# Seven instead of eight block products for three pairs of feed-forward blocks, in a two-model kernel on one core

## The chip, the cores and the metric

The kernel runs on one core of a Trainium2 chip. What counts is the time of one execution on the device in microseconds (us), as the median of several runs. The core has TensorE (matmuls, PE in the profile), VectorE (DVE), ScalarE (ACT), GpSimd (POOL) and SyncE (SP), which here only issues loads. Each engine works through its own list of instructions in order and waits on semaphores for the others.

## The reference

The input is x with 256 tokens of 1024 features, all in float32. Two models are run one after the other: a block with a gated delta rule beside sliding-window attention, then a feed-forward network; and two layers, one with a short convolution and one with dilated attention, each followed by a feed-forward network; a norm ends it. The three feed-forward networks (FFN 0, 1 and 2 below) are what the change touches. Each has a hidden width of 2816:

```
h   = rms_norm(x) * weight                 # 256 tokens x 1024
ffn = (silu(h @ w_gate) * (h @ w_up)) @ w_down
x   = x + ffn                              # FFN 0: x + gate2 * ffn
```

## The kernel before

**Three matmuls for one product.** Every float32 operand is split in two parts of a shorter format (fp32r): high = copy(value), low = value - high. A product is high*high + high*low + low*high, three matmuls into one bank of PSUM. Activations are split once. Weights are split as they arrive: ScalarE's `hi(w)` (L706) copies a tile of 128x2048 from `raw` to `w_hi`, VectorE's `lo(w)` (L1121) subtracts into `w_lo`.

**Loads.** The weights lie in one stream of blocks of 1 MB (128x2048). `raw` has three slots. SyncE's load number i waits until load i-3 has been consumed (`lo_ready`, or `mod_accumulated` for blocks that belong to the modulation of the first model) and then fills its slot. The split tiles have five places: slots 0, 1, 2 in `w_hi`/`w_lo` and 3, 4 in `w_hi2`/`w_lo2`; `FORMER` names the tile whose matmuls must be over (`block_used`) before `hi(w)` may overwrite a place.

**An FFN.** The hidden width is cut in 11 blocks j of 256. For a block, `gate_up(f, j, t)` computes gate and up columns side by side (512 columns) for each half t of the tokens: 8 pieces k of the contraction, 3 matmuls each, so 24 matmuls of 512 columns into bank B[t]. ScalarE applies silu (L968), VectorE multiplies with up (L1598 or L1601). `turn_hid` transposes the result (4 PE instructions, L2371) into bank B[2], ScalarE and VectorE split it (`hid_high` L973, `hid_low` L1606), and `token_rows` multiplies it with block j of w_down: 24 matmuls of 512 columns. The order on TensorE is gate_up(j, 0), gate_up(j, 1), down block j-1 with turn_hid(j) in its middle. The weight tiles of block j+1 are split meanwhile: `lo` on VectorE goes down j-1, gate j+1, product, up j+1, product, hid_low. In FFN 0 VectorE also adds up four more blocks of the stream (`accumulate`, L1143 to L1147), their column sums on TensorE make the last modulation (gate2).

GpSimd does little in the FFNs; at the start of FFN 0 its queue loads two tables for the dilated attention (`t5`, L670 and L671), which the attention after FFN 1 reads.

## Time and profile before

| | |
|---|---|
| median of 3 runs | 980.93 us (980.77 to 981.27) |
| the profiled execution, its time | 981.34 us |
| its span in the trace | 979.5 us |
| PE busy | 971.1 us, 99% |
| DVE busy | 602.9 us, 62% |
| ACT busy | 476.6 us, 49% |
| FFN 0, 1, 2 begin at about | 203, 492 and 790 us of the span |

Busy time says how long an engine had an instruction in work; the granted TensorE clock was full (1.00) in the FFNs. The two numbers of the profiled execution differ by what lies outside of the first and last instruction, 1.8 us.

### The profile page before, as it was taken

How to read it: one execution, taken by the hardware profiler on the slowest of the kernel's cores; microseconds unless marked ns; L12 is line 12 of the kernel's file. 1: busy time of each engine (PE TensorE's matmuls, PEld its weight loads, DVE VectorE, ACT ScalarE, POOL GpSimd, SP SyncE). 2: the span in 40 equal slices, each digit the busy share in tenths (PEclk: the TensorE clock that was granted, in tenths of full speed). 3: DMA queues.
4: the chain of work that ended last, by engine and by line, in shares of the span. 5: the costliest groups of instructions: out<-in, count | busy, mean ns of one | idle time of the engine just before them, and what ended most of it. 6: DMA issues, size and time to landing. Idle time of an engine off the chain costs nothing.

```text
span 979.5 us, 15623 instructions
## 1 busy us (share of the span) xinstructions
PE 971.1 (99%) x6694; PEld 841.1 (86%) x6694; DVE 602.9 (62%) x741; ACT 476.6 (49%) x647; POOL 39.8 (4%) x40
## 2 busy tenths in 40 slices
PE   9999999999999999999999999999999999999998
PEld 6799999988888888999888888889999888888886
DVE  2697988765564545876755455456867663635444
ACT  3584376563443435543454344446555564434343
POOL 0000660010000000000000000000000000000000
...
GB/s 341 292 259 269 73 66 224 263 251 229 239 265 207 177 207 175 173 179 209 172 172 145 240 133 238 148 219 154 223 143 138 157 133 168 198 189 175 211 86 43
DMA packets 32020, 185.70 MB, mean 190 GB/s; under 512 B 3088, under 2 KB 5584, under 8 KB 11600
## 3 DMA queue, kind: packets, MB, share of 16 engines
q1 hardware_dynamic: 30416, 180.37, 51.4%
...
q14 instruction: 15, 0.12, 0.0%
HBM read 183.62 MB, written 1.07 MB: 189 GB/s over the span
## 4 chain that ended last, share of the span: by engine, by line
PE 97%; ACT 1%; DVE 1%; issue 0%; POOL 0%; DVEq 0%; ACTq 0%; POOLq 0%
PE bank L1762 51%; PE acc L1762 43%; PE bank L2371 1%; PE bank L2151 1%; ACT w_hi L706 0%; PE acc L1864 0%; PE bank L1864 0%; ACT probsT L882 0%; ACT X_inv L906 0%; PE acc L2379 0%; ACT inv_b L863 0%; PE bank L2044 0%; DVE norm_tmp L1169 0%; ACT inv_b L874 0%; DVE w_lo L1243 0%
## 5 line engine op out<-in xcount | busy, mean ns | idle before, releaser
L1121 DVE TENSOR_TENSOR w_lo<-raw,w_hi 128x2048 fp32r<-128x2048 f32 x143 | 324.6, 2289 | 144.7 <-ACT w_hi L706 144.6
L1762 PE MATMUL bank<-w_hi,h_parts 128*128 128x512 f32 x1056 | 333.6, 391 | 0.0
L706 ACT ACTIVATE w_hi<-raw 128x2048 fp32r<-128x2048 f32 x143 | 269.7, 1909 | 101.9 <-PE acc L1762 71.4
L1762 PEld LDWEIGHTS bank<-w_hi,h_parts 128*128 128x128 f32 x1056 | 198.4, 188 | 42.6 <-DVE h_parts L1198 1.5
L1762 PE MATMUL bank<-w_lo,h_parts 128*128 128x512 f32 x528 | 205.7, 390 | 0.0
L1762 PE MATMUL acc<-h_parts,w_hi 128*128 128x256 f32 x928 | 170.1, 286 | 0.7 <-DVE h_parts L1173 0.7
L1762 PEld LDWEIGHTS acc<-h_parts,w_hi 128*128 128x128 f32 x928 | 142.8, 189 | 5.5 <-issue 2.4
L1762 PE MATMUL acc<-h_parts,w_lo 128*128 128x256 f32 x464 | 131.2, 283 | 0.0
L1762 PE MATMUL acc<-w_hi,o_hi 128*128 128x512 f32 x296 | 119.2, 403 | 0.0
L1762 PEld LDWEIGHTS bank<-w_lo,h_parts 128*128 128x128 f32 x528 | 99.3, 188 | 19.9
L1762 PE MATMUL acc<-w_hi,o_lo 128*128 128x512 f32 x296 | 115.7, 391 | 0.0
L1762 PE MATMUL acc<-w_lo,o_hi 128*128 128x512 f32 x296 | 115.7, 391 | 0.0
L1762 PEld LDWEIGHTS acc<-h_parts,w_lo 128*128 128x128 f32 x464 | 87.7, 189 | 0.0
L968 ACT ACTIVATE silu_and_hid<-bank,rms 128x256 f32<-128x256 f32 x44 | 20.9, 475 | 105.4 <-PE bank L1762 105.4
L1606 DVE TENSOR_TENSOR o_lo<-bank,o_hi 128x512 fp32r<-128x512 f32 x33 | 22.8, 691 | 75.7 <-ACT o_hi L973 75.7
L1762 PEld LDWEIGHTS acc<-w_hi,o_lo 128*128 128x128 f32 x296 | 55.6, 188 | 12.3
L1762 PEld LDWEIGHTS acc<-w_hi,o_hi 128*128 128x128 f32 x296 | 55.7, 188 | 10.8 <-issue 0.2
L1762 PEld LDWEIGHTS acc<-w_lo,o_hi 128*128 128x128 f32 x296 | 55.8, 188 | 10.5
L973 ACT ACTIVATE o_hi<-bank 128x512 fp32r<-128x512 f32 x33 | 19.8, 599 | 75.0 <-PE bank L2371 75.0
L1598 DVE SCALAR_TENSOR_TENSOR silu_and_hid<-bank,rms,silu_and_hid 128x256 f32<-128x256 f32 x44 | 21.2, 481 | 37.1 <-ACT silu_and_hid L968 37.1
L1762 PE MATMUL bank<-h_parts,w_hi 128*128 128x256 f32 x192 | 35.0, 286 | 0.0
L1762 PEld LDWEIGHTS bank<-h_parts,w_hi 128*128 128x128 f32 x192 | 29.8, 191 | 0.3 <-issue 0.3
...
## 6 DMA issues: line engine op xcount, KB each, us to landing
raw<-stream SPq DMA_DIRECT2D x159, 1024.0 KB, 5.0
...
AT<-stream SPq DMA_DIRECT2D x2, 1024.0 KB, 11.3
qkT<-stream SPq DMA_DIRECT2D x2, 1024.0 KB, 12.7
X_inv<-stream SPq DMA_DIRECT2D x2, 1024.0 KB, 13.7
...
t_tables<-t_scratch POOLq DMA_DIRECT2D x1, 2048.0 KB, 10.3
...
```

Source lines behind the costliest of these rows:

```text
L706: act.activation(high_of(w), raw_of(r), ACT.Copy).then_inc(s.hi_ready, 1)
L968: act.activation(sg[:, T * t:T * t + T], B[t][:, 0:256], ACT.Silu, scale=rms[:, t:t + 1] if f else 1.0).then_inc(s.silu_ready, 1)
L973: act.activation(hid_parts(j)[0].rearrange("p a b -> p (a b)"), B[2][:, :], ACT.Copy).then_inc(s.hid_hi_ready, 1)
L1121: dve.tensor_tensor(low_of(w), raw_of(weight_load(w)), high_of(w), ALU.subtract).then_inc(s.lo_ready, 1)
L1598: dve.scalar_tensor_tensor(out=o, in0=up, scalar=rms[:, t:t + 1], in1=gate, op0=ALU.mult, op1=ALU.mult).then_inc(s.hid_ready, 1)
L1606: dve.tensor_tensor(low.rearrange("p a b -> p (a b)"), B[2][:, :], high.rearrange("p a b -> p (a b)"), ALU.subtract).then_inc(s.hid_lo_rea ...
L1762: return pe.matmul(o, l, r, start=start, stop=stop, skip_group_check=True)
L2151: ins = pe.transpose(bank[hh][:, P * i:P * i + P], sc[:, hh, P * i:P * i + P], perm)
L2371: ins = pe.transpose(B[2][:, T * i + P * t:T * i + P * t + P], hid[:, T * t + P * i:T * t + P * i + P], ident)
```

## The change

Blocks (2, 3), (5, 6) and (8, 9) of each FFN become pairs; blocks 0, 1, 4, 7 and 10 stay as they are. For a pair, the activations form a 2x2 matrix of blocks (two halves of the tokens by two halves of the contraction, 128 tokens x 512), and so do the weights of gate and, apart from them, of up: two halves of the contraction by (gate of both blocks, up of both blocks), each 512x512, which is again a tile of 128x2048. A 2x2 by 2x2 product takes eight block products; Winograd's form takes seven, with sums of blocks before and after:

- a block product (`pair_part(f, q, n)`, n = 0 to 6) is 4 pieces k of 3 matmuls of 512 columns: 12 matmuls.
- Activation sums are made once for each FFN: `mix_second_tokens` and `mix` on VectorE (8 instructions of 128x512), then a copy each on ScalarE (`mixed_high_parts`) and a subtraction each on VectorE (`mixed_lows`) for the four sums.
- Weight sums are made for each pair, in `chain[0]` (in the memory of the t5 tables) and `chain[1]` (in that of x): SyncE loads one quarter of the weights to each (`load_first`, `load_second`); `add_up` adds chain[1] to chain[0]; `add_high_up` adds a block in `raw` to both; and for the last product GpSimd's queue adds a quarter from memory onto chain[0] by a DMA with an addition (`add_weights`), which waits for the low part of product 3 (P3 below). So P0, P2, P3 and P6 are split from states of chain[0], P5 from chain[1], P1 and P4 from `raw`.
- Results: P0 is copied out (`product_copy(0)`) before P3, P5 and P6 are added onto the same bank B[3]; VectorE forms `gate_sum`, `up_sum(0)` (after P3; P5 waits for it), `up_sum(1)` (after P5; P6 waits for it) and the products `pair_product(0)` and `pair_product(1)`, ScalarE two silus of 512 columns.

A pair needs seven split tiles where two blocks needed four. The order of the tiles, `BODY`, is now the order of the splits on ScalarE and VectorE and of the loads. TensorE's order for pair q = (a, b) is P0, turn_hid(a-1), P1, P2, [down a-2 if q > 0], P3, P4, P5, down a-1, P6, gate_up(b+1, 0), turn_hid(a), gate_up(b+1, 1), turn_hid(b), down a. The t5 tables are loaded after FFN 1's last pair. In FFN 0 the four modulation blocks of the stream are accumulated ahead of the low parts of down 2 and down 5 and, for down 4 and down 7, ahead of up_sum(0).

The core of the diff (new functions in full where the prediction speaks of them):

```diff
+PAIRS = ((2, 3), (5, 6), (8, 9))
+SINGLES = (0, 1, 4, 7, 10)
+def pair_steps(q, first, second):
+    return [("pair", q, 0), ("pair", q, 1), ("pair", q, 2)] + first + [("pair", q, 3), ("pair", q, 4), ("pair", q, 5)] \
+        + second + [("pair", q, 6)]
+def gate_steps(j):
+    return [("gate", j), ("up", j)]
+def downs(*js):
+    return [("down", j) for j in js]
+BODY = gate_steps(0) + gate_steps(1) + downs(0) + pair_steps(0, [], downs(1)) \
+    + gate_steps(4) + downs(2) + pair_steps(1, downs(3), downs(4)) \
+    + gate_steps(7) + downs(5) + pair_steps(2, downs(6), downs(7)) + gate_steps(10)
+MADE = BODY + downs(8, 10, 9)
+USED = BODY + downs(8, 9, 10)
...
+MODS_LATE = {(0, "down", 2): 20, (0, "down", 4): 21, (0, "down", 5): 22, (0, "down", 7): 23}
...
+PAIR_SLOTS = ((0, 1, 3, 4, 0, 1, 3), (4, 3, 0, 1, 4, 3, 0), (1, 0, 3, 4, 1, 0, 3))
...
+def shared(v, w):
+    if (kind_of(v) == "pair") == (kind_of(w) == "pair"):
+        return SLOT[v] == SLOT[w]
+    return SLOT[v] // 3 == SLOT[w] // 3 and 2 not in (SLOT[v], SLOT[w])
+FORMER = {w: max((v for v in range(w) if shared(v, w)), key=lambda v: STEP[v], default=None) for w in range(N_TILES)}
...
+            def load_first(f, q):
+                if f + q == 0:
+                    sp.wait_ge(s.x_ready, 8)
+                    sp.wait_ge(s.mod_summed, 2)
+                sp.wait_ge(s.lo_ready, pair_tile(f, q - 1, 6) + 1 if q else FIRST_CHAINS[f])
+                sp.dma_start(halves_of(chain[0]), quarter(f, q, 0, 0)).then_inc(side_landed[0], 16)
+            def load_second(f, q):
+                sp.wait_ge(s.lo_ready, pair_tile(f, q - 1, 5) + 1 if q else FIRST_CHAINS[f])
+                if f + q == 0:
+                    sp.wait_ge(s.t_ready, 8 * 2)
+                    sp.wait_ge(s.xt_psum, 4)
+                sp.dma_start(halves_of(chain[1]), quarter(f, q, 1, 0)).then_inc(side_landed[1], 16)
...
+            def add_weights(f):
+                for q in range(N_PAIRS):
+                    pool.wait_ge(s.lo_ready, pair_tile(f, q, 3) + 1)
+                    pool.dma_start(halves_of(chain[0]), quarter(f, q, 0, 1), accum_op=ALU.add).then_inc(s.rows_added, 16)
+            add_weights(0)
...
+            def mix_second_tokens(f):
+                s1, _, _, s3 = mixed_parts
+                dve.wait_ge(s.h_lo_ready, 8 * (2 * f + 1) + KD)
+                rows_of(f, s1, 1, 4)
+                rows_of(f, s3, 1, 0)
+                dve.tensor_tensor(s1, s1, s3, ALU.subtract).then_inc(s.operands_added, 1)
+            def mix(f):
+                s1, s2, s4, s3 = mixed_parts
+                rows_of(f, s2, 0, 0)
+                dve.tensor_tensor(s3, s2, s3, ALU.subtract).then_inc(s.operands_added, 1)
+                dve.wait_ge(s.operands_added, SUMS * f + 2)
+                dve.scalar_tensor_tensor(out=s2, in0=s1, scalar=-1.0, in1=s2, op0=ALU.mult, op1=ALU.subtract).then_inc(s.operands_added, 1)
+                rows_of(f, s4, 0, 4)
+                dve.wait_ge(s.operands_added, SUMS * f + 3)
+                dve.scalar_tensor_tensor(out=s4, in0=s2, scalar=-1.0, in1=s4, op0=ALU.mult, op1=ALU.subtract).then_inc(s.operands_added, 1)
...
+            def add_up(f, q):
+                dve.wait_ge(side_landed[1], 16 * (pair_count(f, q) + 3))
+                dve.wait_ge(s.lo_ready, pair_tile(f, q, 0) + 1)
+                dve.tensor_tensor(chain[0], chain[0], chain[1], ALU.add).then_inc(s.operands_added, 1)
+            def add_high_up(f, q):
+                r = weight_load(pair_tile(f, q, 4))
+                dve.wait_ge(*landed_of(r))
+                dve.wait_ge(s.lo_ready, pair_tile(f, q, 2) + 1)
+                dve.tensor_tensor(chain[0], chain[0], raw[:, r % RING, :], ALU.add).then_inc(s.operands_added, 1)
+                dve.tensor_tensor(chain[1], chain[1], raw[:, r % RING, :], ALU.add).then_inc(s.operands_added, 1)
...
+                made(("down", 0))
+                silu(f, 0, 1)
+                mixed_high_parts(f, (0,))
+                products(0, 0)
+                mixed_high_parts(f, (3, 1, 2))
+                silu(f, 1, 0)
+                hid_high(f, 0)
+                products(0, 1)
+                silu(f, 1, 1)
+                products(0, 2)
+                for q, (a, b) in enumerate(PAIRS):
+                    if q:
+                        made(("down", a - 2))
+                        products(q, 3)
+                    product_copy(f, q, 0)
+                    hid_high(f, a - 1)
+                    if q:
+                        products(q, 4, 5)
+                        pair_silu(f, q, 0)
+                        product_copy(f, q, 1)
+                    else:
+                        products(q, 3, 4)
+                        product_copy(f, q, 1)
+                        products(q, 5)
+                        pair_silu(f, q, 0)
+                    made(("down", a - 1))
+                    products(q, 6)
+                    made(("gate", b + 1), ("up", b + 1), ("down", a))
+                    pair_silu(f, q, 1)
+                    if q < N_PAIRS - 1:
+                        products(q + 1, 0)
+                        silu(f, b + 1, 0)
+                        hid_high(f, a)
+                        products(q + 1, 1)
+                        silu(f, b + 1, 1)
+                        hid_high(f, b)
+                        products(q + 1, 2)
+                made(("down", JF - 1))
...
+                def made(*steps):
+                    for step in steps:
+                        if (f,) + step in MODS_LATE:
+                            accumulate(MODS_LATE[(f,) + step])
+                        lo(AT_STEP[(f,) + step])
...
+                if f == 0:
+                    made(("gate", 1))
+                made(("up", 1))
+                product(f, 0, 0)
+                mix_second_tokens(f)
+                product(f, 0, 1)
+                mix(f)
+                made(("down", 0))
+                product(f, 1, 0)
+                hid_low(f, 0)
+                products(0, 0)
+                add_up(f, 0)
+                mixed_lows(f)
+                products(0, 1)
+                product(f, 1, 1)
+                products(0, 2)
+                add_high_up(f, 0)
+                for q, (a, b) in enumerate(PAIRS):
+                    if q:
+                        made(("down", a - 2))
+                        products(q, 3)
+                        hid_low(f, a - 1)
+                        gate_sum(f, q)
+                        products(q, 4, 5)
+                        if f == 0:
+                            accumulate(MODS_LATE[f, "down", a - 1])
+                        up_sum(f, q, 0)
+                    else:
+                        gate_sum(f, q)
+                        products(q, 3, 4, 5)
+                        up_sum(f, q, 0)
+                        hid_low(f, a - 1)
+                    lo(down_block(f, a - 1))
+                    pair_product(f, q, 0)
+                    products(q, 6)
+                    up_sum(f, q, 1)
+                    made(("gate", b + 1), ("up", b + 1))
+                    pair_product(f, q, 1)
+                    made(("down", a))
+                    if q < N_PAIRS - 1:
+                        products(q + 1, 0)
+                        add_up(f, q + 1)
+                        product(f, b + 1, 0)
+                        hid_low(f, a)
+                        products(q + 1, 1)
+                        product(f, b + 1, 1)
+                        hid_low(f, b)
+                        products(q + 1, 2)
+                        add_high_up(f, q + 1)
+                made(("down", JF - 1))
```

## Rows read from the trace of the kernel before

**Rows 1.** The page: busy time of the engines, and the chain that ended last.
```profile
PE 971.1 (99%) x6694; PEld 841.1 (86%) x6694; DVE 602.9 (62%) x741; ACT 476.6 (49%) x647; POOL 39.8 (4%) x40
...
PE 97%; ACT 1%; DVE 1%; issue 0%; POOL 0%; DVEq 0%; ACTq 0%; POOLq 0%
```

**Rows 2.** Busy time in 50 us of FFN 1, instructions in brackets.
```profile
600.00:650.00 50.00, 50.00 (x228) 41.38 (x227) 25.07 (x18) 20.77 (x19) 0.00 (x0) 1.00 0.53 189
```

**Rows 3.** Instructions in order of time, ScalarE, FFN 1: start, us.
```profile
537.34 0.47 ACT L968 ACTIVATE silu_and_hid<-bank,rms 128x256 f32<-128x256 f32 x1 [1.66 <-PE bank L1762]
...
542.78 0.47 ACT L968 ACTIVATE silu_and_hid<-bank,rms 128x256 f32<-128x256 f32 x1 [3.16 <-PE bank L1762]
...
554.15 0.47 ACT L968 ACTIVATE silu_and_hid<-bank,rms 128x256 f32<-128x256 f32 x1 [1.66 <-PE bank L1762]
```

**Rows 4.** Groups by line and form, 550 to 650 us: count, busy us, mean ns.
```profile
L1121 DVE TENSOR_TENSOR w_lo<-raw,w_hi 128x2048 fp32r<-128x2048 f32 x18 | 40.7, 2290 | 25.9 <-ACT w_hi L706 25.9
...
L706 ACT ACTIVATE w_hi<-raw 128x2048 fp32r<-128x2048 f32 x19 | 35.7, 1908 | 15.7 <-PE acc L1762 15.7
...
L1598 DVE SCALAR_TENSOR_TENSOR silu_and_hid<-bank,rms,silu_and_hid 128x256 f32<-128x256 f32 x12 | 5.8, 480 | 8.1 <-ACT silu_and_hid L968 8.1
...
L1606 DVE TENSOR_TENSOR o_lo<-bank,o_hi 128x512 fp32r<-128x512 f32 x6 | 4.1, 692 | 16.8 <-ACT o_hi L973 16.8
L973 ACT ACTIVATE o_hi<-bank 128x512 fp32r<-128x512 f32 x6 | 3.6, 599 | 16.1 <-PE bank L2371 16.1
```

**Rows 5.** VectorE in order of time, around the start of FFN 1.
```profile
490.20 0.16 DVE L1588 TENSOR_TENSOR ms<-piece_sums 128x2 f32<-128x2 f32 x1
490.40 0.17 DVE L1589 TENSOR_SCALAR ms<-ms 128x2 f32<-128x2 f32 x1
...
495.27 0.48 DVE L1598 SCALAR_TENSOR_TENSOR silu_and_hid<-bank,rms,silu_and_hid 128x256 f32<-128x256 f32 x1
498.28 0.48 DVE L1598 SCALAR_TENSOR_TENSOR silu_and_hid<-bank,rms,silu_and_hid 128x256 f32<-128x256 f32 x1 [2.53 <-ACT silu_and_hid L968]
500.08 4.49 DVE L1121 TENSOR_TENSOR w_lo<-raw,w_hi 128x2048 fp32r<-128x2048 f32 x2 [1.32 <-ACT w_hi L706]
504.49 0.48 DVE L1598 SCALAR_TENSOR_TENSOR silu_and_hid<-bank,rms,silu_and_hid 128x256 f32<-128x256 f32 x1
504.88 0.68 DVE L1606 TENSOR_TENSOR o_lo<-bank,o_hi 128x512 fp32r<-128x512 f32 x1
```

**Rows 6.** ScalarE in order of time, the first two blocks of FFN 1.
```profile
497.77 0.47 ACT L968 ACTIVATE silu_and_hid<-bank,rms 128x256 f32<-128x256 f32 x1 [3.02 <-PE bank L1762]
...
503.21 0.48 ACT L968 ACTIVATE silu_and_hid<-bank,rms 128x256 f32<-128x256 f32 x1 [1.36 <-PE bank L1762]
...
509.14 0.47 ACT L968 ACTIVATE silu_and_hid<-bank,rms 128x256 f32<-128x256 f32 x1 [3.09 <-PE bank L1762]
```

**Rows 7.** ScalarE in order of time, the start of FFN 0.
```profile
214.66 0.43 ACT L968 ACTIVATE silu_and_hid<-bank 128x256 f32<-128x256 f32 x1
214.92 1.97 ACT L706 ACTIVATE w_hi<-raw 128x2048 fp32r<-128x2048 f32 x1
...
220.10 0.38 ACT L968 ACTIVATE silu_and_hid<-bank 128x256 f32<-128x256 f32 x1 [1.01 <-PE bank L1762]
```

**Rows 8.** The page's DMA queue and issues: KB each, us to landing.
```profile
q1 hardware_dynamic: 30416, 180.37, 51.4%
...
t_tables<-t_scratch POOLq DMA_DIRECT2D x1, 2048.0 KB, 10.3
...
t_tables<-t_scratch POOLq DMA_DIRECT2D x1, 1024.0 KB, 12.6
```

**Rows 9.** DMA issues from 203 to 395 us, FFN 0.
```profile
raw<-stream SPq DMA_DIRECT2D x37, 1024.0 KB, 5.2
```

**Rows 10.** GpSimd's groups by line: the first table load.
```profile
L670 POOL DMA_DIRECT2D t_tables<-t_scratch x1 | 1.2, 1225 | 56.5 <-PE bank L1762 56.5
```

**Rows 11.** VectorE in order of time, FFN 0: two accumulated modulation blocks.
```profile
236.19 0.75 DVE L1143 TENSOR_SCALAR scores<-raw,c_act_sb 128x1024 f32<-128x1024 f32 x1
236.97 1.28 DVE L1147 SCALAR_TENSOR_TENSOR scores<-raw,c_act_sb,scores 128x1024 f32<-128x1024 f32 x1
...
253.01 1.28 DVE L1145 SCALAR_TENSOR_TENSOR scores<-raw,c_act_sb,scores 128x1024 f32<-128x1024 f32 x1
254.32 1.28 DVE L1147 SCALAR_TENSOR_TENSOR scores<-raw,c_act_sb,scores 128x1024 f32<-128x1024 f32 x1
```

**Rows 12.** ScalarE in order of time, FFN 0: a split that waited for its load.
```profile
241.27 1.92 ACT L706 ACTIVATE w_hi<-raw 128x2048 fp32r<-128x2048 f32 x1 [3.47 <-DMA raw<-stream]
243.09 0.36 ACT L968 ACTIVATE silu_and_hid<-bank 128x256 f32<-128x256 f32 x1
```

444 lines of the change are left out of this document (326 added, 118 removed).

## The prediction

> **What bounds the kernel now.** I read the page first: TensorE is busy for 99% of the span and 97% of the chain that ended last lies on it; VectorE is at 62%, ScalarE at 49% [rows 1]. Then the busy time of a stretch inside FFN 1: TensorE without a gap at full clock, VectorE busy half of it, the DMA engines about half [rows 2]. So in the FFNs a matmul taken away shortens the kernel, until one of the other queues comes too late. The third view is the instructions in order of time. Two silus that wait for the two halves of a gate_up stand at 537.34 and 542.78: 24 matmuls of 512 columns in 5.44 us, 0.227 us each. From 537.34 to 554.15, 16.81 us, lies one whole block: 72 matmuls (16.32) and four transposes, 0.49 us [rows 3]. In that time VectorE does three splits, two products and a hid_low, and it idles before each for ScalarE, which waits for TensorE [rows 4].
>
> **What TensorE saves.** A pair has 7 x 12 = 84 matmuls of 512 columns where two blocks had 96. 12 x 0.2267 = 2.72 us a pair, nine pairs: 24.5 us. Down blocks and transposes stay. A block product is then 2.72 us, a down block or half a gate_up 5.44.
>
> **What the other engines get.** A stretch of one pair and one single block takes TensorE 17 x 12 = 204 matmuls (46.3 us) and three groups of transposes, 47.8 us. VectorE does in it 12 splits and 3 weight sums. Two splits in a row take 4.49 us [rows 5], so 2.2 us each back to back; a sum has the same shape with both inputs in SBUF, so I take the same: 33 us. Six instructions of 512 columns for the pair and three hid_low at 0.6 us (691 ns, of which 0.1 overlaps) and two products at 0.4 [rows 4, 5] make 6.2: 39 of 47.8 us. ScalarE: 12 splits of 1.8 to 1.9, seven evictions of 0.6, two silus: 28 us. By busy time nothing binds. What decides is order, so I walked the three queues through the diff with these durations. An instruction that waits for its predecessor's result costs 0.04 us beyond its duration (0.16 us and the next start 0.20 later [rows 5]), so 0.73 for 512 columns.
>
> **Term A, the first pair of each FFN starts late.** In FFN 1, gate_up(0, 1) ends at 497.75, gate_up(1, 0) at 503.2, gate_up(1, 1) at 509.1 [rows 6]. TensorE then has down 0 (514.6), P0, transposes (517.8), P1, P2: it is ready for P3 at 523.2. VectorE finishes product(0, 1) at 498.7, as before [rows 5], since it waits for that silu. Behind it stand, in this order: mix, five instructions (3.4), down 0 (2.2), product (0.4), hid_low (0.6), P0 (2.2), add_up (2.3), four mixed_lows (2.4), P1 (2.2), product (0.4), P2 (2.2), two sums (4.5), gate_sum (0.6), P3 (2.3): 25.7 us, so P3's low part is ready at 524.4. Stall 1.2 us. FFN 2 starts alike: 1.2. In FFN 0 ScalarE now splits down 0 ahead of silu(0, 1): the split at 214.92 takes until 216.9 [rows 7], product(0, 1) ends at 217.7, P3 is ready at 243.3, while TensorE, whose gate_up(0, 1) ended at 214.6, arrives at 240.1. Stall 3.2. A = 5.6 us. None of this work had to be ahead of a matmul before; its cover was the idle half of VectorE.
>
> **Term B, P6 waits for GpSimd's addition.** Count from the moment t when P3's low part is ready and P3 starts. TensorE: P3, P4, P5, down 1, P6 take 16.3 us, then gate_up(4) wants both its tiles. VectorE's queue from t: P4, P5, up_sum(0), hid_low, down 1, pair_product(0) (1.3), P6, up_sum(1), gate 4, up 4: 16.5. So 0.2 us of stall without any wait. But the addition is issued only at t; if it lands L later, P6's split on ScalarE and VectorE (1.9 + 2.3) ends at t + L + 4.2, and up_sum(1), gate and up follow (5.2): the stall is the larger of 0.2 and L - 6.9. Everything behind P6 on ScalarE (gate 4, up 4, down 2, pair_silu(1)) waits with it. No row shows a DMA that adds. The nearest: a plain load of 1 MB lands after 5.2 us [rows 9]; the same queue's second table load of 1 MB took 12.6 us, behind its first (2 MB, 10.3) [rows 8]. Between them I choose: q1 moved 180.37 MB in 51.4% of the span, 503 us, so 1.05 MB takes 2.9 us of transfer and the plain load 2.3 besides; if adding makes two passes over the data, L = 1.2 (issue on GpSimd [rows 10]) + 5.8 + 2.3 = 9.3 us. The Trainium skill ("DMA: Bandwidth & Descriptors", Rules for kernel authors) says that an accumulating DMA reads its destination and writes it later; no row here shows that. With L = 9.3 the stall is 2.4 us in each first pair, B = 7.2 (0.6 if L is 7 or less, 17.1 at 12.6).
>
> In the second and third pair there is room. With time 0 at the start of gate_up(b+1, 0), VectorE ends P3's low part at about 25 and P6 is due on TensorE at 45.1; gate can't be split before P5 is over (39.6) anyway. The same walk gives a stall only from L = 13 on.
>
> **Term C, FFN 0's modulation blocks push down 2 and down 5 back.** The ring holds three loads, and block 20 stands right ahead of down 2 in it; so down 2's load waits for the low part of gate 4 (three loads earlier), where in FFN 1 and 2 it waits for down 1. Gate 4's low part is ready 2.3 us ahead of gate_up(4, 0); the load lands 5.2 later [rows 9], at +2.9. Before the change such a split waited in the same way, but 3.5 us of ScalarE's idle time covered it [rows 12]. Now pair_silu(1) stands behind it on ScalarE: split to 4.8, silu to 5.4. On VectorE pair_product(1) (0.4), block 20 (2.0 [rows 11]), down 2, P0, add_up, product, hid_low(2) end 10.1 later, at 15.5; turn_hid(3) needs that and is due at 5.44 + 0.49 + 5.44 = 11.4. Stall 4.1 us. At down 5 gate 7 is split 4.0 ahead and block 22 takes 2.5 [rows 11]: 14.3, stall 2.9. C = 7.0 us. If loads slow to 7 us beside the chains' loads, C is 10.6; if the two loads land in 4, 4.6.
>
> **At nothing.** The t5 tables, moved behind FFN 1's last pair, have over 30 us (gate_up(10), three down blocks, turn) against 12.6 + 1.2 [rows 8, 10]; without that cover the overhang would be added whole. GpSimd's queue holds nothing else at that point; the next FFN's first addition comes much later. SyncE: load_second and load_first stand ahead of loads whose own waits end later, so they hold nothing up; two more loads and one addition for two fewer raw loads a stretch (7 + 2 + an addition counted twice) add up to about 11 x 2.9 = 32 of 47.8 us of transfer. The split down 9, put last, is ready 1 to 2 us ahead of its use.
>
> **Sum.** -24.5 + A 5.6 + B 7.2 + C 7.0 = -4.7. The profiled execution took 981.3 us, so 976.6; its time is 0.4 above the median of the runs, so 976.2 on their scale. I call 976.
>
> **The rivals.**
> *The addition is quick.* L is 7 us or less: B = 0.6, sum -11.3, 969.6 us. For it: a plain load lands in 5.2 us. Against: it shares the DMA engines with up 4's load and chain[1]'s, issued 2 and 5 us behind it, and the queue's own rows are 10 us and more. By the Trainium skill ("DMA: Bandwidth & Descriptors", Anatomy of one DMA, SWDGE path) a plain transfer from this queue takes about 2.0 us + bytes/436 GB/s, an estimate of 4.4 us for 1 MB; by that the time would be this rival's. The table loads [rows 8] are far slower, but of short rows.
> *The queues hold.* My walk adds durations in strict order; if VectorE runs a few us ahead of it, A and C nearly go: -24.5 + about 4, so 957 to 966, 961 us. For it: VectorE is idle for half of the time now. Against: the two places are long unbroken chains with durations from rows.
> *GpSimd's addition decides.* Each us of L beyond 6.9 costs three times, beyond 13 nine times. -24.5 + 5.6 + 7.0 leaves 11.9 us, so the break-even is L = 10.9. At 12.6 us (the queue's slowest row) B = 17.1 and the time 986.1; at 16 us B is 27.3, the six other pairs add 18, and it is above 1010. For it: 12.6 us has been seen on this queue for the same bytes, and here 2 MB more are in flight. Then the kernel is slower.
>
> **Chances.** The forecast (971 to 979) 0.35; quick addition (966 to 971) 0.23; queues hold 0.12; addition decides 0.23; the terms cancel within 0.2% (979 to 983) 0.07. 0.2% is 2 us, about what these runs can tell from no change. Faster 0.70, same 0.07, slower 0.23. The range leaves out the best part of the second rival and the far part of the third: 962 to 990; it holds both bounds of C and L up to 12.6.
>
> **What would show it.** PE: 108 fewer matmuls, same 0.227 us. A: in each FFN PE waits for VectorE's w_lo just ahead of the first P3, longest in FFN 0. B: from the low part of P3 to the landing of the addition 9 us; ScalarE's split of P6 waits for a DMA; PE idles ahead of gate_up(4, 0). C: in FFN 0 alone, PE waits ahead of the transposes of blocks 3 and 6, ScalarE's down 2 and 5 splits for raw. Wrong would make it: L far from 9, a weight sum that takes more than 2.3 us, or loads slower than 5.2 us under 10 MB a stretch.

## The result, and the profile after

The kernel with pairs takes 992.32 us (median of 4 runs, 990.76 to 993.44), the kernel before in the same session 981.1: ratio 1.0113, 95% interval 1.0097 to 1.0129. It is slower by 1.1%; the prediction was 976 us with a range of 962 to 990, so the time lies 2.3 us beyond the slow end. The profiled execution has a span of 991.6 us against 979.5, so the trace has 12.1 us to explain.

The page: busy time, the chain that ended last, the granted TensorE clock over the span in 40 slices, and the DMA issues (KB each, us to landing).

```profile
PE 955.2 (96%) x6586; PEld 823.6 (83%) x6586; DVE 761.7 (77%) x849; ACT 536.7 (54%) x686; POOL 50.6 (5%) x49
...
PEclk9999999999989999999999999999999999999999
...
PE 75%; DVE 11%; DMA 6%; issue 4%; ACT 3%; SPq 0%; DVEq 0%; ACTq 0%; POOLq 0%
...
raw<-stream SPq DMA_DIRECT2D x141, 1024.0 KB, 5.3
t_tables<-stream SPq DMA_DIRECT2D x9, 1024.0 KB, 5.7
x_res<-stream SPq DMA_DIRECT2D x9, 1024.0 KB, 9.2
t_tables<-stream POOLq DMA_DIRECT2D x9, 1024.0 KB, 10.8
```

The reader is to see four things beside [rows 1]. TensorE has the 108 matmuls less. A quarter of the chain now lies off TensorE, where 3% did. The last line is new: the nine additions land after 10.8 us. And one slice of the clock row, 273 to 297 us in FFN 0, is an 8.

In the steady part of FFN 1 the change does what it says. This is the same 50 us of the span as [rows 2]: TensorE has no gap, VectorE is at 84%.

```profile
600.00:650.00 50.00, 50.00 (x228) 41.36 (x227) 42.14 (x28) 28.75 (x22) 1.19 (x1) 1.00 0.66 210
```

Between the silus of gate_up(4, 0) and gate_up(7, 0) lie 47.67 us; 47.8 was worked out.

**Where the time went.** I cut the span at the silu(0, 1) of FFN 1 (497.77 before [rows 6], 513.47 after) and of FFN 2 (795.74 and 809.05), and at the end. Each piece holds one FFN and should be 3 x 2.72 = 8.16 us shorter; what it lacks of that is its stalls. So FFN 0 has 15.70 + 8.16 = 23.9 us of stalls, FFN 1 (295.58 against 297.97) 5.8 and FFN 2 with the end (182.55 against 183.76) 7.0. Together 36.6 - 24.5 = 12.1, the whole difference. The prediction had 19.8, of which 12.6 in FFN 0. This account is the yardstick for every kernel below. It comes from one profiled execution of each; executions of one kernel differ by up to 5.8 us (e16 below), and the profiled one lies up to 2.3 us off its median, so a difference of 2 us between two accounts shows nothing by itself.

**Term A in the trace.** TensorE around P3 of the first pair in FFN 0:

```profile
239.90 0.39 PE L2171 MATMUL bank<-w_lo,mixed_high 128*128 128x512 f32 x1
240.13 0.39 PE L2171 MATMUL bank<-w_hi,mixed_low 128*128 128x512 f32 x1
243.47 0.75 PE L2171 MATMUL bank<-w_hi,mixed_high 128*128 128x512 f32 x1 [2.95 <-DVE w_lo L1414]
244.01 0.63 PE L2171 MATMUL bank<-w_lo,mixed_high 128*128 128x512 f32 x1
244.44 0.63 PE L2171 MATMUL bank<-w_hi,mixed_low 128*128 128x512 f32 x1
...
246.99 0.39 PE L2171 MATMUL bank<-w_hi,mixed_low 128*128 128x512 f32 x1
247.22 0.40 PE L2171 MATMUL bank<-w_hi,mixed_high 128*128 128x512 f32 x1
```

P3 starts at 243.47 (243.3 was worked out). But look at the distance of the starts: 0.23 us before the gap, 0.43 after it, 0.23 again from 246.99 on. The wait cost its 2.95 us and then another 1.6 at the lower clock level. Windows of 5 us show it (the third number from the end is the granted clock), here and around two longer waits of FFN 0:

```profile
240.00:245.00 5.00, 2.05 (x7) 1.35 (x6) 5.00 (x4) 5.00 (x6) 1.23 (x1) 0.85 0.00 0
245.00:250.00 5.00, 5.00 (x20) 4.00 (x19) 4.70 (x5) 1.76 (x1) 0.00 (x0) 0.80 0.90 147
250.00:255.00 5.00, 5.00 (x24) 4.14 (x23) 2.89 (x3) 0.05 (x1) 0.00 (x0) 1.00 1.01 333
280.00:285.00 5.00, 2.86 (x9) 2.50 (x10) 5.00 (x6) 1.74 (x2) 0.00 (x0) 0.61 0.26 92
285.00:290.00 5.00, 5.00 (x17) 3.94 (x17) 4.33 (x3) 0.66 (x1) 0.00 (x0) 0.71 0.62 210
335.00:340.00 5.00, 1.51 (x7) 1.36 (x8) 4.89 (x5) 0.85 (x2) 0.00 (x0) 0.91 0.50 193
340.00:345.00 5.00, 5.00 (x18) 4.01 (x17) 4.78 (x5) 1.55 (x1) 0.00 (x0) 0.75 0.59 211
```

Of the two levels of 1.2 and 2.4 GHz, 0.61 is a stretch mostly at the lower one. The Trainium skill ("TensorE: Matmul & The Clock Gate", Part 1) calls half rate the default that activity lifts. These windows agree as to the level, and the prediction had no term for it.

**Term B in the trace.** L is the time from the issue of the addition to its landing. FFN 1: GpSimd issues the addition, ScalarE waits for it with P6's split and then does gate 4, up 4 and down 2 in a row.

```profile
540.53 1.19 POOL L881 DMA_DIRECT2D t_tables<-stream  x1 [131.47 <-DVE w_lo L1414]
```
```profile
551.39 1.92 ACT L931 ACTIVATE w_hi<-t_tables 128x2048 fp32r<-128x2048 f32 x1 [7.63 <-DMA t_tables<-stream]
553.21 5.50 ACT L931 ACTIVATE w_hi<-raw 128x2048 fp32r<-128x2048 f32 x3
```

L = 551.39 - 540.53 = 10.9 us, where I had chosen 9.3. TensorE pays ahead of P6, which waits for up_sum(1) behind P6's own low part, and then ahead of gate_up(4, 0). First FFN 1, then FFN 2, each with a 5 us window of the clock:

```profile
556.37 0.47 PE L2171 MATMUL bank<-w_hi,h_parts 128*128 128x512 f32 x1 [2.19 <-DVE probsT L1952]
555.00:560.00 5.00, 3.63 (x11) 2.96 (x12) 5.00 (x4) 3.71 (x3) 0.00 (x0) 0.76 0.75 261
```
```profile
852.89 0.47 PE L2171 MATMUL bank<-w_hi,h_parts 128*128 128x512 f32 x1 [3.14 <-DVE probsT L1952]
857.20 0.50 PE L2171 MATMUL bank<-w_hi,h_parts 128*128 128x512 f32 x1 [1.32 <-DVE w_lo L1414]
850.00:855.00 5.00, 2.10 (x9) 1.80 (x10) 5.00 (x4) 5.00 (x3) 0.00 (x0) 1.00 0.68 242
```

In FFN 1 the clock is at the lower level from 557.6 to 561.0, behind a wait of 2.19 us, and P6's slower matmuls use up the wait at gate_up(4, 0). In FFN 2 it stays at 1.00 behind a wait of 3.14 us. So the length of a wait alone doesn't tell in these rows whether the clock falls.

**Term C in the trace.** FFN 0: two chain and weight loads leave SyncE's queue (L761 is down 2's), then ScalarE, then VectorE and TensorE.

```profile
259.22 0.38 SPq L769 DMA_DIRECT2D t_tables<-stream  x1
262.02 0.33 SPq L761 DMA_DIRECT2D raw<-stream  x1
```
```profile
269.09 1.91 ACT L931 ACTIVATE w_hi<-raw 128x2048 fp32r<-128x2048 f32 x1 [8.62 <-DMA raw<-stream]
270.91 0.58 ACT L1223 ACTIVATE probsT<-bank 128x512 f32<-128x512 f32 x1
```
```profile
271.59 0.69 DVE L1966 TENSOR_TENSOR probsT<-probsT 128x512 f32<-128x512 f32 x1 [7.39 <-ACT probsT L1223]
...
281.31 0.68 DVE L1971 TENSOR_TENSOR o_lo<-bank,o_hi 128x512 fp32r<-128x512 f32 x1
```
```profile
272.33 0.66 PE L2813 MATMUL bank<-consts,probsT 128*128 128x128 f32 x4 [2.31 <-DVE probsT L1966]
282.14 1.08 PE L2813 MATMUL bank<-consts,probsT 128*128 128x128 f32 x4 [3.68 <-DVE o_lo L1971]
```

The load lands 7.0 us after its issue, not 5.2; pair_silu(1) (L1223) stands behind the split; VectorE idles for 7.4 us before the pair's product; and TensorE waits at both turns of the pair (a turn is the group of transposes of `turn_hid`). The same happens at down 5, whose load lands after 7.3 us: TensorE waits 1.36 and 4.21 us there. The four waits are 11.6 us.

### The profile page after: what moved, and what is told of

It is laid out like the page before. It is cut to its first block, busy times and chain, and to the rows that moved or that the text cites. A ratio compares the mean times of both kernels' runs of the same rounds, so it can differ in the third digit from the quotient of the medians.

```text
span 991.6 us, 15642 instructions
## 1 busy us (share of the span) xinstructions
PE 955.2 (96%) x6586; PEld 823.6 (83%) x6586; DVE 761.7 (77%) x849; ACT 536.7 (54%) x686; POOL 50.6 (5%) x49
## 4 chain that ended last, share of the span: by engine, by line
PE 75%; DVE 11%; DMA 6%; issue 4%; ACT 3%; SPq 0%; DVEq 0%; ACTq 0%; POOLq 0%
PE acc L2171 37%; PE bank L2171 35%; DVE w_lo L1414 5%; DMA t_tables<-stream 3%; ACT w_hi L931 2%; DMA raw<-stream 1%; DMA X_inv<-stream 1%; PE bank L2813 1%; DVE mixed_low L1925 1%; DVE x_res L1940 1%; PE bank L2560 1%; PE acc L2273 0%; PE bank L2273 0%; DVE o_lo L1971 0%; DVE norm_tmp L1486 0%
## 5 line engine op out<-in xcount | busy, mean ns | idle before, releaser
L1414 DVE TENSOR_TENSOR w_lo<-raw,w_hi 128x2048 fp32r<-128x2048 f32 x125 | 284.2, 2285 | 37.8 <-ACT w_hi L931 37.6
L2171 PE MATMUL bank<-w_hi,h_parts 128*128 128x512 f32 x696 | 227.0, 397 | 8.9 <-DVE probsT L1952 6.3
L2171 PEld LDWEIGHTS bank<-w_hi,h_parts 128*128 128x128 f32 x696 | 131.3, 189 | 40.3 <-DVE w_lo L1414 11.6
L2171 PE MATMUL bank<-w_lo,h_parts 128*128 128x512 f32 x348 | 136.2, 392 | 0.0
L1414 DVE TENSOR_TENSOR w_lo<-t_tables,w_hi 128x2048 fp32r<-128x2048 f32 x36 | 82.3, 2286 | 19.1 <-ACT w_hi L931 19.0
L931 ACT ACTIVATE w_hi<-t_tables 128x2048 fp32r<-128x2048 f32 x36 | 68.9, 1913 | 48.8 <-DMA t_tables<-stream 41.0
L2171 PEld LDWEIGHTS bank<-w_lo,h_parts 128*128 128x128 f32 x348 | 65.8, 189 | 12.5
L2171 PEld LDWEIGHTS acc<-w_hi,o_hi 128*128 128x128 f32 x296 | 56.7, 192 | 11.6 <-issue 0.2
L2171 PEld LDWEIGHTS acc<-w_lo,o_hi 128*128 128x128 f32 x296 | 56.5, 191 | 11.3
L2171 PE MATMUL bank<-w_hi,mixed_high 128*128 128x512 f32 x144 | 57.1, 397 | 5.7 <-DVE w_lo L1414 5.7
L2171 PE MATMUL bank<-w_lo,mixed_high 128*128 128x512 f32 x144 | 56.7, 394 | 0.0
L2171 PE MATMUL bank<-w_hi,mixed_low 128*128 128x512 f32 x144 | 56.5, 392 | 0.0
L881 POOL DMA_DIRECT2D t_tables<-stream x9 | 10.8, 1205 | 642.2 <-DVE w_lo L1414 642.2
## 6 DMA issues: line engine op xcount, KB each, us to landing
t_tables<-stream POOLq DMA_DIRECT2D x9, 1024.0 KB, 10.8
AT<-stream SPq DMA_DIRECT2D x2, 1024.0 KB, 11.8
```

Of the source, the lines that this page charges most:

```text
L881: pool.dma_start(halves_of(chain[0]), quarter(f, q, 0, 1), accum_op=ALU.add).then_inc(s.rows_added, 16)
L931: act.activation(split_tile((w_hi, w_hi2), w), split_source(w), ACT.Copy).then_inc(s.hi_ready, 1)
L1414: dve.tensor_tensor(split_tile((w_lo, w_lo2), w), split_source(w), split_tile((w_hi, w_hi2), w), ALU.subtract).then_inc(s.lo_ready, 1)
L2171: return pe.matmul(o, l, r, start=start, stop=stop, skip_group_check=True)
```

## The experiments

Theory T: the loss is terms B (the addition's landing) and C (modulation blocks ahead of down 2 and 5), both mis-sized, and the clock around their waits. Rivals: the added weight sums make VectorE's queue the limit as such (V), or the order of splits is what costs (O). In the tables the stalls are those of the account above, from each kernel's profiled execution.

### Each suspect alone

Modulation blocks ahead of other down blocks (e1_mods_later):

```
-MODS_LATE = {(0, "down", 2): 20, (0, "down", 4): 21, (0, "down", 5): 22, (0, "down", 7): 23}
+MODS_LATE = {(0, "down", 3): 20, (0, "down", 4): 21, (0, "down", 6): 22, (0, "down", 7): 23}
```

> FFN 0's modulation blocks 20 and 22 are loaded and accumulated ahead of down 3 and down 6 instead of down 2 and down 5; nothing else moves. Theory 1 (my term C, undersized): the late load of down 2 and down 5 holds pair_silu(1) up, and with it the transposes; from the end of the first P6 on FFN 0 loses 15.7 us in the changed kernel's trace. They go: some 15 us faster than the changed kernel, 976 to 979 us, and the two ScalarE waits for raw of 8 us in FFN 0 vanish. Rival (VectorE and the DMA engines are simply too full in FFN 0, so the work waits wherever it stands): 5 us or less, 987 us or more.

Without the fourth sum (e2_no_last_sum); P6 is then split from chain[0] as it was for P3, a sum that lacks the last quarter:

```
-                    pool.wait_ge(s.lo_ready, pair_tile(f, q, 3) + 1)
-                    pool.dma_start(halves_of(chain[0]), quarter(f, q, 0, 1), accum_op=ALU.add).then_inc(s.rows_added, 16)
+                    pass
...
-                    elif n:
-                        act.wait_ge(s.rows_added, 16 * pair_count(f, q) + 16)
-                    else:
+                    elif n == 0:
```

> GpSimd's addition is left out in all nine pairs, and P6 is split from chain[0] as it stands (so P6 multiplies the wrong sum; all else is computed). Theory 1 (my term B with a landing of 10.9 us): in each first pair the stall ahead of gate_up(4, 0) falls from about 4.5 to 0.2 us, and with it the slower clock behind it in FFN 1; the other pairs don't change: 13 to 15 us faster than the changed kernel, 977 to 979 us. Rival (the stall is VectorE's own queue, or the queue behind it has no room either): 5 us or less, 987 us or more.

The same transfer as a plain copy (e3_plain_load); P6 is the product of the last quarter alone:

```
-                    pool.dma_start(halves_of(chain[0]), quarter(f, q, 0, 1), accum_op=ALU.add).then_inc(s.rows_added, 16)
+                    pool.dma_start(halves_of(chain[0]), quarter(f, q, 0, 1)).then_inc(s.rows_added, 16)
```

> The same transfer from GpSimd's queue without the addition (a plain copy onto chain[0]; P6 multiplies a quarter instead of a sum). If adding costs a second pass over the data (my working of 9.3 us), it lands 2.9 us sooner, after some 8 us. If the queue itself and the traffic beside it set the time, it lands after 10 to 11 us as now.

pair_silu(1) ahead of the down block's split on ScalarE (e4_silu_first):

```
-                    made(("gate", b + 1), ("up", b + 1), ("down", a))
+                    made(("gate", b + 1), ("up", b + 1))
                     pair_silu(f, q, 1)
+                    made(("down", a))
```

> On ScalarE pair_silu(1) stands ahead of the split of down a instead of behind it; nothing else moves. Theory 1 (term C: the late load of down 2 and down 5 holds pair_silu(1) back): TensorE's wait ahead of turn_hid(a) goes, and the one ahead of turn_hid(b) shrinks, since only VectorE's split of down a still waits for the load: 3 to 4 us for each of the two places in FFN 0, 984 to 986 us. Rival (what holds turn_hid(b) is VectorE's chain of splits and sums alone): no change, 991 us or more.

Both cures at once, e1's and e2's edits, so that P6 again lacks the last quarter (e5_mods_no_sum):

> Both single cures at once: the modulation blocks moved off down 2 and down 5, and no addition by GpSimd's queue (P6 is then split from one quarter alone and is not the product of the sum). If terms B and C are two separate losses, their gains add: 992.3 - 12.6 - 14.9 = 964.8, so 963 to 967 us. That would leave -24.5 + 5.6 (A) = -18.9 predicted against about -16 measured, A with its share of slower clock. If both runs cured the same waits (a slower clock, or the order of VectorE's queue as a whole), the gains overlap and the time stays at 970 to 977.

Zero matmuls in TensorE's waits of FFN 0, into banks that are overwritten next (e9_fill), in the first two pairs, 10 ahead of the first turn and 14 ahead of the second (the first is shown):

```
                     gate_up(f, b + 1, 0)
+                    if f == 0 and q < 2:
+                        for _ in range(10):
+                            mm(B[1][:, :], zero_r[:, 0:P], zero_r[:, :], True, True)
                     turn_hid(f, a)
...
```

> In FFN 0, TensorE does 10 matmuls of zeros in a free bank ahead of turn_hid(a) and 14 ahead of turn_hid(b) for the first two pairs, 2.3 and 3.2 us, where it waits 2.5 and 3.5 us. Everything that is computed stays. Theory (the waits bring the granted clock down, 0.61 and 0.71 in the 10 us behind the second of them, and the half speed is lost on top of the wait): the clock stays at 1.00 there and 4 to 6 us come back, 987 us. Rival (the slower matmuls stand where TensorE has to wait anyway): same time, within 1 us, or slower by what the zeros run over.

| kernel | median us | ratio to before | stalls FFN 0, 1, 2 |
|---|---|---|---|
| the change | 992.32 | 1.0113 | 23.9, 5.8, 7.0 |
| e1, blocks moved | 979.69 | 0.999 (0.9981 to 0.9999) | 10.8, 5.6, 6.8 |
| e2, no fourth sum | 977.39 | 0.9965 (0.9954 to 0.9977) | 17.9, 1.6, 1.5 |
| e3, plain copy | 977.08 (one run) | | 16.6, 1.6, 2.0 |
| e4, silu first | 983.01 | 1.0026 (1.0015 to 1.0037) | 11.2, 5.9, 8.1 |
| e5, e1 and e2 | 965.55 | 0.9844 (0.983 to 0.9859) | 4.2, 1.7, 1.6 |
| e9, filler | 988.66 | 1.0082 (1.0065 to 1.0099) | 19.0, 5.5, 6.8 |

T holds and the two losses are separate: e5 fell into the 963 to 967 us expected of two gains that add. C is in FFN 0 alone: 13.1 us go there with the blocks moved, 13.7 when the sum is gone too (12.6 and 11.8 by the medians). B is in all three: 6.0 + 4.1 + 5.4 = 15.5 (14.9 by the medians). The silu's place takes away 12.7 us of FFN 0 in the account, 9.3 by the medians (the change's profiled execution was its slowest, e4's one of its fastest): it is the other end of the same chain, and TensorE still waits 2.72 and 1.73 us at the second turns, where hid_low stands behind the late split on VectorE. The plain copy equals no sum at all, so what costs is the adding, not the transfer; its row is

```profile
t_tables<-stream POOLq DMA_DIRECT2D x9, 1024.0 KB, 6.1
```

With L = 6.1 my formula max(0.2, L - 6.9) gives no wait, and there is none. The filler gives back 4.9 us of FFN 0 in the account and 3.7 by the medians. It makes no operand ready earlier; what changed is the granted clock behind the turns, 1.00 in these windows where the change had 0.61 to 0.91:

```profile
280.00:285.00 5.00, 4.50 (x23) 3.50 (x22) 4.88 (x7) 2.41 (x2) 0.00 (x0) 1.00 0.22 42
285.00:290.00 5.00, 5.00 (x24) 4.09 (x23) 4.90 (x3) 2.49 (x2) 0.00 (x0) 1.00 0.46 187
335.00:340.00 5.00, 5.00 (x24) 4.12 (x24) 4.48 (x5) 2.40 (x2) 0.00 (x0) 1.00 0.51 179
340.00:345.00 5.00, 5.00 (x26) 4.14 (x25) 5.00 (x3) 4.35 (x4) 0.00 (x0) 1.00 0.08 31
```

So some 4 to 5 us of C was clock. At term A's wait there was no filler, and the clock fell there too, to 0.69 and 0.63 from 240 to 250 us.

### Other cures of the same causes

Four kernels were meant to keep the result and lose the stalls. Order in the first pair (e7_first_pair): P3 ahead of gate_sum, the second of two sums (`add_high_second`, split off from `add_high_up`) behind P4, silu(0, 1) ahead of down 0's split. VectorE's part, cut:

```
+                        products(q, 3)
                         gate_sum(f, q)
-                        products(q, 3, 4, 5)
+                        products(q, 4)
+                        add_high_second(f, q)
+                        products(q, 5)
```

> In the first pair of each FFN, P3's low part stands ahead of gate_sum and of the second sum, which moves behind P4's low part; and silu(0, 1) stands ahead of the split of down 0. Theory 1 (terms A and B are one chain: VectorE's queue up to P3's low part, then the addition that is issued at that moment): P3's low part comes 2.8 us sooner in FFN 1 and 2 and over 4 in FFN 0, and gate_up(4, 0) with it as long as VectorE's own queue (16.5 us from there, 3 of them moved behind) isn't longer than the addition's: 6 to 9 us faster than the changed kernel, 983 to 986 us. Rival (the addition lands when the DMA engines let it, not 10.8 us after its issue): under 2 us, 990 us or more.

Everything with the addition (e8_all_dma: e1, e4 and e7 together), and the same with the fourth sum on VectorE from a plain load (e10_all_dve):

> The three edits together: modulation blocks at down 3 and down 6, the first pair's order, pair_silu(1) first; GpSimd's queue still adds. Theory 1: the gains of the parts add up where they are at different places (12.6 measured, 6 to 9 expected, the silu's only where a load is still late): 970 to 974 us. Rival (a stall removed at one place returns at the next, VectorE and DMA being near their limit): 976 us or more.

> As the kernel before in this list, but VectorE makes the last sum too, from a fourth raw load, between up_sum(0) and the down split (after P5's low part), and GpSimd adds nothing. Theory 1: in the first pair VectorE's 2.2 us replace a wait of some 4 us for the addition; in the others it has 2.9 us of idle time there, so the sum costs nothing: 0 to 4 us faster than its neighbour, 967 to 972 us. Rival (VectorE is the bound by then): slower than its neighbour by up to 9 x 2.2 = 20 us.

| kernel | median us | ratio to before | stalls FFN 0, 1, 2 |
|---|---|---|---|
| e7, first pair | 992.41 | 1.0122 (1.0105 to 1.0139) | 18.9, 7.3, 7.4 |
| e8, all with addition | 983.07 | 1.0027 (1.0017 to 1.0037) | 13.1, 7.1, 7.4 |
| e10, all on VectorE | 995.58 | 1.0147 (1.0132 to 1.0162) | 19.5, 8.9, 8.6 |

All three missed, and each came out in the time range of its rival; e7's rival, that the DMA engines set the landing, is not what the rows show. VectorE of e7 in FFN 1, and TensorE's wait for its up_sum(0) ahead of P5, say why:

```profile
528.16 2.29 DVE L1941 TENSOR_TENSOR t_tables<-t_tables,raw 128x2048 f32<-128x2048 f32 x1
532.44 2.29 DVE L1416 TENSOR_TENSOR w_lo<-t_tables,w_hi 128x2048 fp32r<-128x2048 f32 x1 [1.99 <-ACT w_hi L933]
...
537.44 2.29 DVE L1948 TENSOR_TENSOR x_res<-x_res,raw 128x2048 f32<-128x2048 f32 x1
541.71 2.29 DVE L1416 TENSOR_TENSOR w_lo<-x_res,w_hi 128x2048 fp32r<-128x2048 f32 x1 [1.98 <-ACT w_hi L933]
```
```profile
544.75 0.62 PE L2182 MATMUL bank<-w_hi,mixed_high 128*128 128x512 f32 x1 [4.12 <-DVE probsT L1960]
```

A sum and the low part of its own tile have ScalarE's split of 1.9 us between them. With two sums and gate_sum in a row that split ran while VectorE did other work; with each tile right behind its sum, VectorE idles for 2.0 us twice. P3's low part came only 0.6 us sooner in FFN 1, not 2.8, and P5 waits. The addition was not the reason: it was issued at 535.03, and ScalarE's split of P6 began 8.98 us later without a wait for it. So this other order of the first pair is worse by 1.5 us in FFN 1 and 0.5 in FFN 2. FFN 0 has 5.0 us less of stalls in e7's profiled execution, but that one was 1.8 us below e7's median and the change's 1.1 above its own. The order of the first pair is not what made the change slow; that the order matters, e10 shows below.

Next, each part on top of the moved blocks (all four kernels below have e1's edit). The silu first (e11), the fourth sum on VectorE with the old order, behind up_sum(0) in the first pairs (shown) and ahead of it in the others (e12), silu(0, 1) ahead of down 0's split (e13):

```
+            def add_last(f, q):
+                r = weight_load(pair_tile(f, q, 6))
+                dve.wait_ge(*landed_of(r))
+                dve.wait_ge(s.lo_ready, pair_tile(f, q, 3) + 1)
+                dve.tensor_tensor(chain[0], chain[0], raw[:, r % RING, :], ALU.add).then_inc(s.operands_added, 1)
...
                         up_sum(f, q, 0)
+                        add_last(f, q)
                         hid_low(f, a - 1)
                     lo(down_block(f, a - 1))
```

> Modulation blocks moved and, besides, pair_silu(1) ahead of the split of the down block on ScalarE, in all nine pairs; the addition stays. If the split of down 2 or 5 still makes that silu late once the modulation blocks are gone, the time falls 2 to 4 us below the 979.7 of the moved blocks alone: 976 to 978. If the moved blocks had taken away all of that chain, it stays at 979 to 980. If the reordering itself is what cost time in the two kernels with everything changed at once, it rises above 981.

> Modulation blocks moved; the fourth weight sum is made by VectorE, in front of up_sum(0), from a fourth plain load into the ring; nothing is left on GpSimd's queue. VectorE has 2.3 us more a pair, but the load can be issued early. If the landing of the addition is what B is, and VectorE's idle time of about 20% hides the 2.3 us, the time is 966 to 971. If VectorE's queue is already the limit between P3 and gate_up(b+1), the stall goes from the landing to the queue: 2.3 us more in each of nine pairs less what the landing cost: 977 to 985. It also says whether the 995.6 of the kernel with everything on VectorE came from this sum (then over 985) or from the order that it also had.

> Modulation blocks moved, and silu(0, 1) put ahead of the split of down 0 on ScalarE. In FFN 0 that split of 1.9 us stood ahead of the silu; the queue of VectorE up to P3 is then 2 us shorter there, in FFN 1 and FFN 2 nothing changes. Term A in FFN 0 falls from 3.2 to about 1.2 and the slower clock behind it goes: 976 to 978 us against 979.7. If the late P3 is not what costs there, 979 to 980.

And e12's sum in the first pair of each FFN alone (e16):

> The modulation blocks where they stood in the 979.7 us kernel, VectorE's fourth sum in the three first pairs alone, ScalarE's order untouched. Gain over 979.7: 0.7 + 1.3 + 2.0 = 4.0 us by the stretches measured, so 975 to 977. If it stays at 979 or more, the 983 of the kernel with this sum in all nine pairs was not the work in FFN 0's second and third pair alone.

| kernel | median us | ratio to before | stalls FFN 0, 1, 2 |
|---|---|---|---|
| e11, silu first | 982.75 | 1.0014 (1.0004 to 1.0024) | 12.8, 5.4, 7.0 |
| e12, sum on VectorE | 982.99 | 1.0028 (1.0016 to 1.004) | 16.2, 4.3, 4.9 |
| e13, silu(0, 1) first | 981.15 | 1.0006 (0.9997 to 1.0016) | 11.3, 5.7, 7.0 |
| e16, sum on VectorE in first pairs | 977.12 | 0.9967 (0.9956 to 0.9978) | 13.5, 4.3, 4.6 |

e11 fits blocks and silu as one chain: cured once, the second cure gives nothing. But it also came out above 981, the third case of its expectation: on top of the moved blocks the same reordering costs 3.1 us by the medians (2.0 of stalls in FFN 0). Why it does is not shown. In e12 VectorE's sum costs less than the addition in FFN 1 and 2 (4.3 against 5.6, 4.9 against 6.8) and more in FFN 0's second and third pair: there TensorE's stretches between the turns behind gate_up(4, 0), (7, 0) and (10, 0) are 53.4 and 52.6 us, against 50.9 and 48.3 with the addition (e1) and 48.0 and 48.2 with neither (e5). (The silus mislead here: e1's silu of gate_up(10, 0) runs 4.2 us after TensorE has gone on to the turn, behind a split that waited for its load.) V is right there, where VectorE has the modulation blocks too, and in the first pairs: a window of e12 in FFN 1, VectorE's busy time third,

```profile
520.00:549.00 29.00, 25.98 (x116) 20.88 (x115) 28.84 (x19) 14.92 (x11) 0.00 (x0) 1.00 0.47 162
```

shows VectorE busy for 28.84 of 29 us while TensorE lacks 3. The first pair lasts 51.64 us there and 49.00 in e5: 2.6 us for a sum of 2.2 to 2.3, with no cover at all. e12 also tells what e10 was: it has the same sum without e10's two reorderings and is 12.6 us faster, and e10's waits of 4.13 to 4.16 us ahead of P5 in all three first pairs are e7's. With VectorE that full, the order of the splits costs much (O). e16 takes the better choice for each place in FFN 1 and 2 and gets 3.5 us in them, and loses 2.7 in FFN 0 in its account (2.6 us faster by the medians; 975 to 977 was expected). e13 begins the pair 1.8 us earlier and loses 1.4 in it: TensorE's wait at P3 only falls from 2.95 to 2.19 us, so term A in FFN 0 was not the silu's place alone.

### A version that beats both

e14_best: silu first, VectorE's sum in first pairs alone, and one modulation block in each place, none in the first pair.

```
+MODS_LATE = {(0, "down", 4): 20, (0, "down", 5): 21, (0, "down", 7): 22, (0, "down", 8): 23}
```

> Three edits: the modulation blocks of FFN 0 stand ahead of down 4, 5, 7 and 8 (one at each of the second and third pair's middle and end, none in the first); pair_silu(1) ahead of the down block's split on ScalarE; and in the first pair of each FFN alone VectorE makes the fourth sum from a plain load, the other six pairs keep the addition. By the stretches of the single kernels: FFN 0 52.0 + 48.5 + 49.6 = 150.1 us against 155.9 with the moved blocks, FFN 1 and 2 51.7 and 51.9 for the first pair against 53.0 and 53.9. Together 9 us less than 979.7: 970 to 972. If the losses do not add by place but the order of VectorE's queue is rigid as a whole, as in the two kernels with everything changed, 979 to 983.

e15 keeps the addition everywhere, e17 leaves the silu behind the down block's split, e18 moves only block 20, to down 3:

> The same without VectorE's fourth sum: the addition stays in all nine pairs. FFN 0 about 52.7 + 48.5 + 49.6 = 150.8, FFN 1 and 2 as with the moved blocks (53.0, 53.9): 979.7 - 5 = 974.5, range 973 to 977. The difference to the kernel with VectorE's sum in the first pairs then is 3 to 4 us, the price of the addition where it is not covered less the 2.3 us of VectorE.

> As the first kernel of this batch but with ScalarE's order untouched (the down block's split ahead of pair_silu(1)). With block 21 ahead of down 5 and block 23 ahead of down 8, their loads stand behind a modulation load again, as down 2 did: if term C's mechanism holds, pair_silu(1) is late in the second pair and the time is 3 to 4 us above that kernel: 974 to 976. If the silu's place is worth nothing here, both are equal within 1 us.

> The 976.25 us kernel with only one modulation block moved from where the change had it: block 20 from down 2 to down 3, the others ahead of down 4, 5 and 7 as in the change; pair_silu(1) ahead of the down block's split and VectorE's fourth sum in the first pairs stay. By stretches of FFN 0 in earlier kernels: 52.0 (no block in the first pair), 49.9, and 49.6 with blocks 22 and 23 ahead of down 5 and 7, which is 151.5 against 153.6: 974 to 975. If what a block costs does not depend on its place beyond that, 976 to 977.

| kernel | median us | ratio to before | stalls FFN 0, 1, 2 |
|---|---|---|---|
| e14 | 976.25 | 0.9953 (0.9939 to 0.9967) | 10.0, 4.4, 4.8 |
| e15, addition everywhere | 979.73 | 0.9989 (0.9976 to 1.0003) | 12.3, 5.3, 7.2 |
| e17, silu behind the split | 985.20 | 1.005 (1.0035 to 1.0065) | 20.3, 4.4, 5.2 |
| e18, one block moved | 979.55 | 0.9979 (0.997 to 0.9988) | 14.1, 4.6, 4.4 |

e14 is 16 us faster than the change and 4.4 faster than the kernel before, and still 4 us above the 972 that was expected at most; e15 missed its range by 3. The pair e14 and e17 is the sharpest test of C: one line of ScalarE's order, 9 us, 10.2 of stalls in FFN 0. ScalarE of e17 ahead of the silu of gate_up(7, 0), and then of e14:

```profile
315.11 1.91 ACT L931 ACTIVATE w_hi<-raw 128x2048 fp32r<-128x2048 f32 x1 [9.04 <-DMA raw<-stream]
316.93 0.58 ACT L1223 ACTIVATE probsT<-bank 128x512 f32<-128x512 f32 x1
```
```profile
310.55 0.60 ACT L1223 ACTIVATE probsT<-bank 128x512 f32<-128x512 f32 x1 [4.37 <-PE bank L2180]
313.96 1.92 ACT L931 ACTIVATE w_hi<-raw 128x2048 fp32r<-128x2048 f32 x1 [2.81 <-DMA raw<-stream]
```

pair_silu(1) is 6.4 us earlier; TensorE, not a load, releases it. I had expected 3 to 4 us for it: the size of C was missed a second time in the same direction. e18 missed: its second pair took 54.4 us by the silus where 49.9 were expected. ScalarE waits there 2.6 us for a weight load and 5.9 for the addition:

```profile
296.02 1.92 ACT L931 ACTIVATE w_hi<-raw 128x2048 fp32r<-128x2048 f32 x1 [2.57 <-DMA raw<-stream]
303.87 1.92 ACT L931 ACTIVATE w_hi<-t_tables 128x2048 fp32r<-128x2048 f32 x1 [5.93 <-DMA t_tables<-stream]
```

The addition was issued at 291.4, so L = 12.5 us, with the DMA engines at a share of 1.0 for the whole of 293 to 308. But the change's own addition at 297.8 landed in 10.9 us at the same share, and one of e18 in FFN 1, where there are no modulation blocks, took 12.4; what sets L between 9 us (e7's first pair) and 13.5 (e1) is not shown. On TensorE the late addition costs 0.45 and 1.31 us ahead of P6 and gate_up(7, 0). More is lost at the second turn:

```profile
328.67 0.63 PE L2822 MATMUL bank<-consts,probsT 128*128 128x128 f32 x4 [3.83 <-DVE o_lo L1979]
```

There hid_low stands behind down 5's low part, and ScalarE's split of down 5 waited 6.3 us for its load, with block 22 ahead of it: the half of C that the silu's place doesn't cure. e14 has 1.99 us at this turn.

## Why the prediction was wrong

**TensorE's saving** was right: 108 matmuls, 47.67 us a stretch against 47.8, 24.5 us.

**Term A** held in mechanism and nearly in size: 1.65 and 1.56 us in FFN 1 and 2 of e5, where only A is left (1.4 predicted with the 0.2 that B has without a wait). FFN 0 has 4.2 there against 3.4. In the changed kernel P3 began there when it should, but the starts of eight matmuls behind it were 0.2 us too far apart, 1.6 us in all. The sum is 7.4 against 6.2 (5.6 without the three 0.2).

**Term B** is the first step that failed, by the size of L and by one assumption. The formula comes near: with L of 10.9 in FFN 1 and 11.5 in FFN 2 (issue 836.4, split 847.9), less 6.9 and less the 0.2 that stays anyway, it gives 3.8 and 4.4; taking the sum away gained 4.1 and 5.4. TensorE's idle time stands ahead of P6 first, not ahead of gate_up(4, 0) alone as the signs had it. L was built as a plain transfer of 5.2 plus 2.9 for a second pass and 1.2 for the issue; measured are 6.1 for the plain one with its issue and 4.7 for the adding. The assumption is that the other pairs stall "only from L = 13 on". It is right in FFN 1 and 2 (47.67 to 47.70 us in all four). In FFN 0 the second pair of e1 is 3.0 us longer on TensorE than in e5: its addition lands after 13.5 us, and TensorE waits 1.35 us ahead of P6 and 1.30 ahead of gate_up(7, 0). L had passed the threshold there; that it would, and the size of the stall behind it, were missed. The third pairs differ by 0.1 us. B was 15.5, not 7.2.

**Term C** failed by more: 13.4 against 7.0. The text had the bound, 10.6 "if loads slow to 7 us beside the chains' loads", and the load did land in 7.0; I had taken 5.2 from a trace in which no chain load goes out 2.8 us ahead of it. At down 2 the two waits are 2.31 + 3.68 = 6.0 us, and the walk with 7 us gives 5.9: there the chain was right and the load's time wrong. At down 5 they are 1.36 + 4.21 = 5.6 against 4.7 by the bound. The rest is the clock, 4 to 5 us by the filler. Waits and clock add up to more than 13.4, since the late turns also cover what B costs in the second pair: e1's waits of 1.35 and 1.30 us there are absent in the change.

**The clock** was missing. Every wait was priced at its length, and the trace before has the clock at 1.00 through the FFNs. Sum of what was measured: -24.5 + 7.4 + 15.5 + 13.4 = 11.8, against 12.1 in the trace.

**The rivals.** The addition is quick: no, L is 10.8, though e3 shows that it would be for a plain transfer. The queues hold: no in FFN 0, and e12 shows that VectorE has no slack in the first pairs. GpSimd's addition decides: its break-even was L = 10.9 with A and C as predicted; L in the three first pairs ended at 11.2, 10.9 and 11.5, which alone would have given 1 us more than no change. What made the kernel slower was L and C and the clock together, which no rival had: each moved one or two terms and left the rest at the forecast. The slow end of the range did take L of 12.6 and C of 10.6 together. B stayed below that bound (15.5 against 17.1); A and C did not, by 1.8 and 2.8 us, and what no bound held is the clock.

**Still open:** what sets the landing of the addition, and why e11's reordering costs time. FFN 0's 10 us of stalls in e14 show in its trace for the most part: term A's wait (2.96 us) with the lower clock behind it, 0.40 and 0.74 us in the first pair, where VectorE makes the sum, and 1.99 us at the second turn of the second pair with a lower clock from 325.3 to 328.7; the remainder is not accounted for.
